# Splitting the forms of the first five ff pairs while they are made, and bringing both parts back from DRAM

## What is computed

```
h2 = rmsnorm(x, norm_mlp_g)                              # 520 x 2048
f = jax.nn.relu(jnp.einsum('btd,df->btf', h2, w_up))     # w_up 2048 x 8192
x = x + jnp.einsum('btf,fd->btd', f * f, w_down)         # w_down 8192 x 2048
y = rmsnorm(x, norm_final_g)
```

## Time and profile before

| | |
|---|---|
| median of 3 runs | 1854.97 us (1853.54 to 1855.86) |
| the profiled execution's own time | 1855.15 us |
| its span, first to last instruction | 1853.1 us |
| TensorE busy | 1814.2 us (98%) |
| VectorE busy | 1477.5 us (80%) |
| ScalarE busy | 923.8 us (50%) |
| DMA over the span | 288.21 MB, mean 156 GB/s |
| granted TensorE clock | 0.997 of full speed, mean |

### The profile page before, as it was taken

One profiled execution on the slowest core, in us unless ns is written; L12 is line 12 of the kernel. 1 busy time (PEld: TensorE's weight loads), 2 busy tenths in 40 slices (PEclk: granted clock), 3 DMA queues, 4 the chain that ended last, 5 costly groups with the idle time before them and its releaser, 6 DMA issues. The chain is left out here.

```text
span 1853.1 us, 38289 instructions
## 1 busy us (share of the span) xinstructions
PE 1814.2 (98%) x15016; PEld 1805.6 (97%) x15016; DVE 1477.5 (80%) x2028; ACT 923.8 (50%) x1316; POOL 131.8 (7%) x222
## 2 busy tenths in 40 slices
PE   7999999999999999999999999999999999999997
PEld 6999999999999999999999999899999999999997
DVE  7777785445488888888888888888888888889886
ACT  6545533333344544454454455555555555555554
POOL 2000000200000001000000000110000000000100
PEclk9999999999999999999999999999999999999999
DMA  8333233444345345444444542887666766767632
GB/s 278 97 96 92 91 97 92 127 142 139 113 149 174 133 154 177 151 155 141 166 142 145 174 133 90 246 241 203 182 185 186 199 179 182 198 161 208 206 103 93
DMA packets 209420, 288.21 MB, mean 156 GB/s; under 512 B 9389, under 2 KB 185017, under 8 KB 209248
## 3 DMA queue, kind: packets, MB, share of 16 engines
q1 hardware_dynamic: 185344, 186.86, 32.6%
q0 software_dynamic: 23920, 99.18, 18.7%
HBM read 222.00 MB, written 64.53 MB: 155 GB/s over the span
## 5 line engine op out<-in xcount | busy, mean ns | idle before, releaser
L863 PE MATMUL ps<-forms,u_high 128*128 128x260 f32 x1344 | 379.9, 283 | 2.2 <-ACT u_high L1128 1.2
L865 PE MATMUL ps<-forms,u_low 128*128 128x260 f32 x1344 | 379.5, 282 | 0.0
L864 PE MATMUL ps<-forms,u_high 128*128 128x260 f32 x1344 | 379.2, 282 | 0.0
L863 PE MATMUL ps<-forms,d_high 128*128 128x260 f32 x1120 | 317.1, 283 | 3.1 <-DVE d_low L1737 1.4
L865 PE MATMUL ps<-forms,d_low 128*128 128x260 f32 x1120 | 316.1, 282 | 0.0
L864 PE MATMUL ps<-forms,d_high 128*128 128x260 f32 x1120 | 316.1, 282 | 0.0
L863 PEld LDWEIGHTS ps<-forms,u_high 128*128 128x128 f32 x1344 | 253.0, 188 | 2.5 <-ACT u_high L1128 1.4
L864 PEld LDWEIGHTS ps<-forms,u_high 128*128 128x128 f32 x1344 | 253.4, 189 | 0.0
L865 PEld LDWEIGHTS ps<-forms,u_low 128*128 128x128 f32 x1344 | 252.8, 188 | 0.0
L1277 DVE TENSOR_TENSOR w_low<-raw,w_high 128x512 fp32r<-128x512 f32 x160 | 109.0, 689 | 136.9 <-ACT w_high L941 135.7
L863 PEld LDWEIGHTS ps<-forms,d_high 128*128 128x128 f32 x1120 | 210.7, 188 | 5.1 <-issue 4.3
(11 more groups left out here) (305 smaller groups left out, 4380.3 us busy)
## 6 DMA issues: line engine op xcount, KB each, us to landing
even_rows<-in_w_up_dram SPq DMA_DIRECT2D x32, 1024.0 KB, 5.4
odd_rows<-in_w_up_dram SPq DMA_DIRECT2D x32, 1024.0 KB, 5.7
d_even<-in_w_down_dram SPq DMA_DIRECT2D x33, 768.0 KB, 6.7
d_odd<-in_w_down_dram SPq DMA_DIRECT2D x33, 768.0 KB, 5.2
raw<-in_w_in_dram SPq DMA_DIRECT2D x96, 256.0 KB, 2.7
sums_spill<-part_out POOLq DMA_DIRECT2D x40, 520.0 KB, 5.4
scratch<-f_spill POOLq DMA_DIRECT2D x20, 910.0 KB, 7.1
f_spill<-f_out POOLq DMA_DIRECT2D x32, 520.0 KB, 4.6
```

The source lines that it names most:

```text
L863: pe.matmul(out, wh[:, k, :], xh, start=(PRODUCT_OPENS[r] and k == 0), stop=False, skip_group_check=True)
L864: pe.matmul(out, wh[:, k, :], xl, start=False, stop=False, skip_group_check=True)
L865: mm = pe.matmul(out, wl[:, k, :], xh, start=False, stop=last, skip_group_check=True)
```

## The change

For the first five pairs (`EARLY = 5`) the forms are split in `w_up`. After `f_sums(m)` the forms are not sent at once: `split_high(m)` (ScalarE, in m+1 at turn 6 of 7) copies all 7 forms in the matmul's format into `f_in[0]` (the buffer `scratch`, free in `w_up`), and `split_low(m)` (VectorE, in m+2 at turn 0) subtracts them in place. Even pairs take two operations on each engine, odd pairs three. To make room, `f_scale` and `f_sums` of these pairs go one turn earlier. `send_f` writes both parts to a second DRAM tensor `f_parts_spill`.

`load_early(kp)` brings both parts of a pair back straight into its `f_forms` set: three transfers (forms 0-2, forms 4-6, form 3), 1820 KB in all, with a semaphore each, for which TensorE waits at turn 0, 1 and 6 of the segment that first uses the pair. Pairs 0 and 1 are loaded ahead of `send_f(30)` in GpSimd's list, pairs 2 to 4 behind it. `window_high` and `window_low` of kp 0 to 4 are gone. kp 5 is loaded already during `w_up`. Pair 31 is squared and scaled in segment 1 and summed in segment 3.

```diff
+EARLY, PIECES = 5, ((0, 3), (4, 7), (3, 4))
-FORMS_AT = {first_q(_s) + (6 if _kp == 2 else 3): _kp for _kp, _s in BUILD.items() if _kp >= 2}
-FORMS_AT[UP_Q - 6] = 0
+FORMS_AT = {first_q(_s) + 3: _kp for _kp, _s in BUILD.items() if _kp >= EARLY}
-SQUARES_AT, SCALE_AT, SUMS_SEG = first_q(3) + 3, first_q(3) + 6, 6
+SQUARES_AT, SCALE_AT, SUMS_SEG = first_q(1) + 3, first_q(1) + 6, 3
...
+            def load_early(kp):
+                if kp == 0:
+                    pool.wait_ge(u_lo, UP_Q - PRODUCTS)
+                elif kp == 1:
+                    pool.wait_ge(u_lo, UP_Q)
+                else:
+                    pool.wait_ge(u_used, UP_Q)
+                pool.wait_ge(split_sent, 16 * EARLY)
+                for b in range(2):
+                    pool.wait_ge(f_out_sent[b], SENT[EARLY - 1 - (EARLY - 1 - b) % 2])
+                for piece, (first, end) in enumerate(PIECES):
+                    pool.dma_start(f_forms[kp][:, :, first:end, :].bitcast(F32),
+                                   parts_dram[kp, :, :, first:end, :]).then_inc(early_in[kp][piece], 16)
...
             def send_f(m):
                 pool.wait_ge(f_ready, m + 1)
+                to = parts_dram[m, :, 1] if m < EARLY else f_dram[m]
+                if m < EARLY:
+                    pool.dma_start(parts_dram[m, :, 0], f_in[0]).then_inc(split_sent, 16)
...
                 if m == UP_PAIRS - 2:
-                    load_f(1)
+                    load_early(0)
+                    load_early(1)
                 send_f(m)
                 if m == 8:
-                    load_f(0)
+                    load_f(EARLY)
+            for kp in range(2, EARLY):
+                load_early(kp)
...
+                        if FIRST_USE[kp] == m - UP_PAIRS and kp < EARLY and r in (0, 1, 6):
+                            pe.wait_ge(early_in[kp][(0, 1, 6).index(r)], 16)
...
+            def split_high(m):
+
+                act.wait_ge(f_summed, m + 1)
+                act.wait_ge(split_sent, 16 * m)
+                for part, first, end in split_parts(m):
+                    act.activation(f_in[0][:, first:end, :].bitcast(F32R), part, ACT.Copy).then_inc(split_hi, 1)
...
+            def split_low(m):
+
+                dve.wait_ge(f_summed, m + 1)
+                for n, (part, first, end) in enumerate(split_parts(m)):
+                    dve.wait_ge(split_hi, split_count(m) + n + 1)
+                    if end == FORMS:
+                        settle()
+                    ins = dve.tensor_tensor(part.bitcast(F32R), part, f_in[0][:, first:end, :], ALU.subtract)
...
-                if 1 <= m < UP_PAIRS and r == 5:
+                if 1 <= m < UP_PAIRS and r == (4 if m <= EARLY else 5):
                     f_scale(m - 1)
-                if 1 <= m < UP_PAIRS and r == 6:
+                if 1 <= m < UP_PAIRS and r == (5 if m <= EARLY else 6):
                     f_sums(m - 1)
```

More of the change, by code:

```diff
@@ L96, in first_q @@
     return UP_Q + PRODUCTS * seg
-_latest, BUILD = {DOWN_KP: LAST}, {0: -2, 1: -1}
-for _kp in reversed(range(2, DOWN_KP)):
+_latest, BUILD = {DOWN_KP: LAST}, {EARLY - 1: -1}
+for _kp in reversed(range(EARLY, DOWN_KP)):
     _latest[_kp] = min(FIRST_USE[_kp], _latest[_kp + 1]) - 1
-_latest[2] -= 1
-for _kp in range(2, DOWN_KP):
+for _kp in range(EARLY, DOWN_KP):
     BUILD[_kp] = max(BUILD[_kp - 1] + 1, _latest[_kp] - (1 if _kp >= D_SETS else 0))
@@ L108, with built @@
     assert BUILD[_kp] <= _latest[_kp]
[L111 to L112 removed]
+def built(kp):
+    return 2 * (kp - EARLY)
+FORMS_AT = {first_q(_s) + 3: _kp for _kp, _s in BUILD.items() if _kp >= EARLY}
 LANDS = [0 if _kp < D_SETS else 1 - _kp % 2 for _kp in range(DOWN_KP)]
[L115 to L118 removed]
+LANDING = [sum(LANDS[_k] == LANDS[_kp] for _k in range(EARLY, _kp + 1)) for _kp in range(DOWN_KP)]
+LANDED_BEFORE = [max((_k for _k in range(EARLY, _kp) if LANDS[_k] == LANDS[_kp]), default=None) for _kp in range(DOWN_KP)]
+SQUARES_AT, SCALE_AT, SUMS_SEG = first_q(1) + 3, first_q(1) + 6, 3
 SENT = {}
@@ L363, in build @@
         f_hi, f_lo = sem("f_hi"), sem("f_lo")
+        f_summed, split_hi, split_sent = sem("f_summed"), sem("split_hi"), sem("split_sent")
+        early_in = [[sem(f"early_in{kp}_{piece}") for piece in range(len(PIECES))] for kp in range(EARLY)]
         sums_sent = [sem(f"sums_sent{b}") for b in range(2)]
@@ L599, in _ @@
                     load_x2(o + 2)
+            def load_early(kp):
[11 more added lines that the diff above has]
+                                   parts_dram[kp, :, :, first:end, :]).then_inc(early_in[kp][piece], 16)
             def load_f(kp):
                 before = LANDED_BEFORE[kp]
-                if kp == 0:
-                    pool.wait_ge(r2_ready, 1)
+                if before is None and LANDS[kp] == 0:
+                    pool.wait_ge(split_sent, 16 * EARLY)
                 elif before is None:
@@ L608, in load_f @@
                 else:
[L609 to L610 removed]
+                    pool.wait_ge(f_hi, built(before) + 2)
+                    pool.wait_ge(f_lo, built(before) + 2)
                 pool.wait_ge(f_out_sent[kp % 2], SENT[kp])
@@ L1240, in _ @@
                 seg = m - UP_PAIRS
-                if turn == UP_Q:
-                    window_high(1, 0)
-                    window_high(1, 1)
                 weights_high(turn)
                 up_copies(turn)
+                if r == 6 and 1 <= m <= EARLY:
+                    split_high(m - 1)
                 for part in range(2):
@@ L1817, in f_sums @@
                 settle()
-                dve.tensor_tensor(s4, a12, s2, ALU.subtract).then_inc(f_ready, 1)
+                dve.tensor_tensor(s4, a12, s2, ALU.subtract).then_inc(f_summed if m < EARLY else f_ready, 1)
+            def split_low(m):
[5 more added lines that the diff above has]
+                    ins = dve.tensor_tensor(part.bitcast(F32R), part, f_in[0][:, first:end, :], ALU.subtract)
+                    if end < FORMS:
+                        step(ins)
+                ins.then_inc(f_ready, 1)
             def window_low(kp, part):
-                dve.wait_ge(f_hi, 2 * kp + part + 1)
+                dve.wait_ge(f_hi, built(kp) + part + 1)
                 a, b = (0, 4) if part == 0 else (4, FORMS)
@@ L1848, in _ @@
                 seg = m - UP_PAIRS
-                if turn == UP_Q:
-                    window_low(1, 0)
-                    window_low(1, 1)
+                if r == 0 and 2 <= m <= EARLY + 1:
+                    split_low(m - 2)
                 if r == 0:
```

37 lines of the change are left out of this document (20 added, 17 removed).

## The result

| | before | changed |
|---|---|---|
| median, 7 runs each on one chip | 1854.97 us (1852.33 to 1857.82) | 1862.52 us (1861.79 to 1863.67) |
| ratio | | 1.004, 95% interval 1.003 to 1.0051 |
| span of the profiled execution | 1853.1 us | 1860.2 us |

The changed kernel is slower, by 7.5 us or 0.4%.

A forecast was written before the change was run, and what follows sets the result against it. TensorE, busy 98%, was taken as the bound, with 13.6 us lost in segments 0 to 7. Segment 3 starting 5.7 us later, less 3.8 us back, gave +1.9 us on 1855.15: 1857.0 us, range 1850.5 to 1863.5.

The forecast's parts named there:

- the sum: Up to segment 3's start 5.7 us later, then 3.8 us back: net +1.9 us, 1857.0 us.
- rival 3: Segments 1, 2: rows under about 60 GB/s, segment 3 from 1200 or later; +5 to +9 us; chance 0.15.
- I take 0: w_up: the added splits fit VectorE's idle gaps, so TensorE loses 0; bounds 0 and 2.2 us a pair, 11 us.
- if w_up lengthens: w_up: sign that would show the forecast wrong; it expected 624.5 us for m 1 to 31, unchanged.
- kp 1's second piece up to 1.2 us late: Load of pair 1: a lateness of up to 1.2 us, allowed for within the forecast's own range, -2 to +6 us.
- Together 3.31 MB or 8.3 us: End of w_up: segment 0's rows, kp 1 and pair 30 move at 400 GB/s; pair 30 has landed at 1169.9.
- 73 GB/s, since that row is the same two kinds of transfer.: Segment 1's rows beside loads of kp 2 to 4: share taken from a late stretch of the trace, 73 GB/s.
- rival 1: Segments 1 and 2: rows get a fair half, 200 GB/s; first send_sums holds instead; -3.5 us, 1851.6; chance 0.2.
- I put their landing at 1189.7: Segment 2's rows: the remaining 0.29 MB share the engines with the first sums and land at 1189.7.
- Segment 1's start at 1177.0 and its turn 1 at 1180.6: Segment 1: starts 1.0 us behind its even rows, at 1177.0; turn 1 waits for odd rows until 1180.6.
- 3.8 us come back: From segment 3 on: of 5.2 us lost before, 0.5 stays for f_sums and 0.9 for kp 5 to 7.
- rival 2: Segments 0 to 7: loads land in time, their bytes hidden; -9.6 us, 1845.5; chance 0.12.

The follow-up runs named there:

- e4: Changed kernel plus 68 and 22 extra unused matmuls before segment 1's first two products, keeping TensorE busy while it waits: 1863.3 us, ratio 1.0045 to before.
- e9: Changed kernel, but pair 1 split in segment 0, pairs 2-4 issued by SyncE behind rows of segments 2-4, pair 31 treated in segments 3 and 4: 1851.36 us.
- e10: Changed kernel with only pairs 2, 3, 4 issued from SyncE's queue behind the rows of segments 2, 3, 4: 1855.81 us, ratio 1.0001 to before.
- e5: Changed kernel with pair 3 loaded behind the first send_sums and pair 4 behind the third: 1862.09 us, ratio 1.0036 to before.

## Why the prediction came out as it did

The direction of the sum and its mechanism were right; two sizes were not, and both made it too small. That the range holds the result is owed to rival 3, which drew its upper end, and not to the sum. The sum's times are those of the trace before. The changed trace came to the same point 0.7 us sooner (SyncE's first rows were issued at 1158.75 against 1159.42), so the misses below are taken with 0.7 us added to its times.

- **"I take 0"** for w_up. Right for the splits: pairs 1 to 30 take 604.33 us in both traces, with VectorE's busy time up from 533.94 to 541.62 us. Pair 31 takes 1.4 us more and segment 0's first turn 1.2 us, so that the text's sign "if w_up lengthens" did appear, but not for the splits. TensorE starts segment 0 at 1166.26 and its second turn at 1168.22; pair 1's first two pieces, issued at 1159.03 and 1159.75, took 7.1 and 8.4 us and landed at 1166.2 and 1168.1. I had this only as "kp 1's second piece up to 1.2 us late", in the forecast's range. It cost little in the end, since segment 1 waited for rows anyhow.
- **"Together 3.31 MB or 8.3 us"**, with pair 30 landed at 1169.9. 2.6 us short: it landed at 1171.8. The engines were slower, and they had more to move. From 1160 to 1169 us they moved 3.05 MB, 339 GB/s, and from 1162 to 1166 only 311 to 332 at a share of 1.01, where I took 400 from another mixture of transfers. And from 1159 to 1171 they moved 3.90 MB: at least 0.55 MB of it belonged to the next loads, issued from 1165.64 on, which passed before the send had landed.
- **"73 GB/s, since that row is the same two kinds of transfer."** This is the step that failed most. 48 GB/s were measured. The text named the longer runs beside the rows of the late stretch as a point for rival 1; it was the other way round. Here the packets of GpSimd's queue were the longer ones, 5.0 KB on the average against 3.7, and the rows got less. So segment 1's rows landed at 1180.7 and 1185.2 instead of 1176.0 and 1179.6, 5.3 and 6.2 us late: 2.6 us of each from the late issue, the rest from the share.
- **"I put their landing at 1189.7"**, of segment 2's rows. They landed at 1188.3 and 1189.3. The whole amount of bytes was sized well, and its division was not.
- **Segment 1's start at 1177.0 and its turn 1 at 1180.6.** The chain was right: 1.0 us behind its even rows, 0.9 us behind its odd ones, at 1181.73 and 1186.10, so 5.4 and 6.2 us later than said. From there to segment 3 the sum gave 16.6 us and the trace has 15.8. The miss of the whole sum, 5.5 us by the medians and 6.0 by the stretch, is already complete at that turn.
- **"3.8 us come back."** 3.1 did: from segment 3 on 2.1 us are lost instead of 5.2, with 1.1 us for f_sums where I had 0.5. Segments 4 to 6 lose nothing, as the text had it.
- **Rival 3** ("if the rows get less than about 60 GB/s ... segment 3 starts at 1200 or later ... 1862") named the condition and the size: 48 GB/s, 1201.9, 1862.5. Two parts of it were wrong. Segment 2's rows were not what held (they had landed 4.6 us before its first product), and the slower clock, 1.7 us a time by the text for 3.4 us of it, cost about 0.6 us for 13.65 us of it, at most some 2 (e4). It had 0.15 of the chance and should have had more: the decisive number was an average from another place, and the condition lay only 13 GB/s below it.
- **Rivals 1 and 2** fell with the share of the rows. e9 shows that something like rival 2 is there to be had, though only 3.9 us of its 9.6, with another order of issue, with pair 1 split on chip and pair 31 treated later.

The Trainium skill (DMA: Bandwidth & Descriptors, Queues, rings and completion order) has each engine take turns between the queues it has work for, one packet at a time. Its packet is a bundle of descriptors, and whether the profile counts the same thing no run here shows. What the traces show agrees in the main: 406 and 294 packets beside 2.03 and 0.29 MB. If packets of 1 KB and 5.0 KB took strict turns, the rows would get a sixth, an estimate of 64 GB/s of 386, and 48 were measured; in the late stretch the same estimate gives 79 of 370 beside packets of 3.7 KB, and 90 were measured. So the size of the packets gives the direction, and the estimate is 16 GB/s too high at one place and 11 too low at the other. No run changed that size alone: that it is the cause is likely and not shown.

## What to carry to other kernels

Work that is moved from an engine to DMA is paid for in the queue: before trusting the bytes' sum, ask which small, urgent transfer passes beside the new large ones, and do not take its share from another stretch, where the packets beside it have another size. Try urgent and patient transfers on one queue in order of need: in e10 and e9 segment 1's rows then landed in 2.8 to 4.0 us. And an experiment that only moves a burst can give the time of the wrong theory (e5): read where the wait went before reading the median.

## What was not expected of the hardware

- Two queues that are both full share the engines very unequally: 338 to 48 GB/s in the changed kernel, from 1174 to 1180 us.
- The first sums, written with accumulation, are dear for their size. In e9 from 1177 to 1183 us (packets, MB, share of the engines):

```profile
q1 hardware_dynamic: 1224, 1.29, 61.5%
q0 software_dynamic: 143, 0.53, 44.2%
```

  0.53 MB hold 44.2% of the engines for 6 us, which is 200 GB/s; the rows and forms beside them move at 350 by the same count.
- 13.65 us at 1.2 GHz cost about 0.6 us, at most some 2 (e4): TensorE had matmuls running in 6.8 of them.
